# PEER picks split between VectorE and ScalarE, a shorter top-16 and an earlier first list of ids

## The reference, cut to what matters

```python
def peer(h, w_query, keys1, keys2, exp_u, exp_v):
    q = (h @ w_query).reshape(T, PEER_HEADS, 2, D_PHALF)
    s1 = jnp.einsum('thd,nd->thn', q[:, :, 0], keys1)
    s2 = jnp.einsum('thd,nd->thn', q[:, :, 1], keys2)
    v1, i1 = lax.top_k(s1, 16)
    v2, i2 = lax.top_k(s2, 16)
    cand_s = v1[..., :, None] + v2[..., None, :]          # 16 x 16 sums
    cand_i = i1[..., :, None] * 128 + i2[..., None, :]
    top_s, sel = lax.top_k(cand_s, 16)
    e_idx = jnp.take_along_axis(cand_i, sel, axis=-1)
    gate = jax.nn.softmax(top_s, axis=-1)
    u = exp_u[e_idx]
    act = jax.nn.gelu(jnp.einsum('thkd,td->thk', u, h))
    return jnp.einsum('thk,thkd->td', gate * act, exp_v[e_idx])
```

## Time and profile before

| | |
|---|---|
| median of three runs | 1144.43 us |
| profiled execution, its own time | 1144.88 us |
| its span, from the first to the last instruction | 1143.1 us |
| TensorE busy | 856.5 us (75%) |
| VectorE busy | 784.8 us (69%) |
| ScalarE busy | 454.8 us (40%) |
| GpSimd busy | 536.3 us (47%) |
| mean granted clock of TensorE | 0.902 |
| moved by the DMA engines | 456.60 MB, 402.68 MB of it by the gathers |

### The profile page before, as it was taken

How to read it: one execution, slowest core, us unless ns; L and a number is a source line. 1 busy time by engine, 2 the same in 40 slices (tenths; PEclk the granted TensorE clock), 3 DMA queues, 4 the chain that set the end, 5 groups by cost and what they waited for, 6 DMA issues and landing times.

```text
span 1143.1 us, 12068 instructions
## 1 busy us (share of the span) xinstructions
PE 856.5 (75%) x3879; PEld 396.3 (35%) x3884; DVE 784.8 (69%) x2005; ACT 454.8 (40%) x1423; POOL 536.3 (47%) x437
## 2 busy tenths in 40 slices
PE   8999988997896858685686777587666756655555
PEld 6748743443232424241243442143223222211111
DVE  2325877876677888796666786757877777667554
ACT  2121454333444334552564663343343333333334
POOL 0002445553555554553553553556564654455442
PEclk9999999999999888897889898889898788887879
DMA  9902999999999999999999999999999999999996
GB/s 375 411 2 70 421 425 425 427 424 430 425 427 425 426 428 426 361 430 422 425 427 425 425 427 427 425 426 427 426 427 426 427 427 428 427 425 427 427 428 269
DMA packets 66791, 456.60 MB, mean 399 GB/s; under 512 B 8227, under 2 KB 10019, under 8 KB 15526
## 3 DMA queue, kind: packets, MB, share of 16 engines
q0 software_dynamic: 55888, 402.68, 83.8%
q1 hardware_dynamic: 10694, 52.87, 11.4%
q10 hardware_dynamic: 144, 0.26, 0.1%
HBM read 451.49 MB, written 3.24 MB: 398 GB/s over the span
## 4 chain that ended last, share of the span: by engine, by line
DMA 48%; PE 26%; DVE 11%; POOL 7%; ACT 4%; issue 3%; SPq 0%; POOLq 0%; DVEq 0%
DMA rows<-in_uv,ids 37%; PE ps L598 25%; DMA wt<-in_uv,ids 8%; DVE rows L2043 6%; POOL rows L537 4%; POOL work L520 2%; DMA wt<-in_uv,last_ids 1%; DMA rows<-in_w_qi 1%; ACT work L1249 1%; ACT wt L1249 1%; DMA wt<-in_w_q 1%; ACT wgt L1249 1%; DVE wt L2043 1%; PE ps L601 1%; ACT zact L1249 1%
## 5 line engine op out<-in xcount | busy, mean ns | idle before, releaser
L537 POOL DMA_INDIRECT rows<-in_uv,ids x352 | 400.3, 1137 | 444.9 <-PE ps L598 360.7
L598 PE MATMUL ps<-rows,work 128*64 128x512 f32 x1416 | 409.4, 707 | 245.2 <-ACT work L1249 239.7
L2043 DVE CUSTOM_DVE_ANT_0 rows<-rows,wt 128x1024 f32<-128x1024 f32 x226 | 276.9, 1225 | 160.9 <-DMA rows<-in_uv,ids 155.7
L1249 ACT ACTIVATE zact<-zdot 128x1 f32<-128x1 f32 x354 | 71.6, 202 | 488.2 <-DVE zdot L2043 480.5
L598 PEld LDWEIGHTS ps<-rows,work 128*64 128x64 f32 x1416 | 96.2, 151 | 479.3 <-ACT work L1249 327.3
L598 PE MATMUL ps<-wt 128*128 128x128 f32 (+6 forms) x719 | 195.9, 476 | 30.4 <-ACT wt L1249 28.1
L2043 DVE CUSTOM_DVE_ANT_0 rows<-rows,masks 128x1024 f32<-128x1024 f32 x128 | 156.3, 1224 | 67.3 <-DMA rows<-in_uv,ids 64.5
L598 PEld LDWEIGHTS ps<-wt 128*128 128x128 f32 (+2 forms) x724 | 97.8, 185 | 106.6 <-issue 58.8
L1249 ACT ACTIVATE work<-pair,wgt 128x64 f32<-128x64 f32 x354 | 123.4, 349 | 11.5
L1249 ACT ACTIVATE wgt<-zact,gates 128x1 f32<-128x1 f32 x354 | 104.5, 295 | 11.6
L598 PEld LDWEIGHTS ps<-work,wt 128*128 128x128 f32 (+1 forms) x664 | 84.2, 202 | 48.6 <-issue 48.2
(11 more groups left out here) (178 smaller groups left out, 722.9 us busy)
## 6 DMA issues: line engine op xcount, KB each, us to landing
wt<-in_w_q SPq DMA_DIRECT2D x7, 2048.0 KB, 15.9
rows<-in_uv,ids POOLq DMA_INDIRECT x352
rows<-in_w_out SPq DMA_DIRECT2D x2, 2048.0 KB, 32.5
wt<-in_w_out SPq DMA_DIRECT2D x2, 2048.0 KB, 12.0
wt<-in_ckv SPq DMA_DIRECT2D x16, 256.0 KB
x<-in_x SPq DMA_DIRECT2D x5, 512.0 KB, 8.9
rows<-in_w_qi SPq DMA_DIRECT2D x1, 2048.0 KB, 13.3
wt<-in_w_qa SPq DMA_DIRECT2D x1, 2048.0 KB, 12.5
```

The costliest lines, as they stand in the source:

```text
L537: pool.indirect_dma_start(row[s], None, a["uv"], bass.IndirectOffsetOnAxis(ap=ids[:, own(n // KP).start + n % KP:own(n // KP).start + n % ...
L598: return nc.tensor.matmul(out, lhsT, rhs, start=start, stop=stop)
L1249: return nc.scalar.activation(*args, **kw)
L2043: V.tensor_tensor_reduce(row[s][:, 0:D], row[s][:, 0:D], h2r[t][:, n % 2, :], 1.0, 0.0, ALU.mult, ALU.add, zdots[s]).then_inc(dotted, 1)
```

## The change

There are three parts.

1. *Picks 250 to 378, the even ones (65 of them).* VectorE runs a plain multiply of two 128x1024 tensors and no accumulator read. ScalarE, at the head of `weigh`, runs a Copy over the 1024 products with an accumulator, waits for it, and goes on with the gelu. `gelus(n)` counts the semaphore for it.
2. *Top-16 of every unit.* The two casts to fp32 go. The index of the first half is shifted left by 7 bits while it is an integer; the place among the 256 candidates is split into its two nibbles by one AND with the constants 240 and 15 (set once at the start) in place of a shift, an AND and a cast; the comparison constants are 0, 16, 32 ... for the first half and 0, 1, 2 ... for the second; and one reduction over both halves gives the id, where a reduction to two half ids and a multiply-add gave it. `post` signals a semaphore and yields, with no wait after.
3. *Unit 0.* Its ids signal `chosen` on their own, ahead of the softmax. `spread_first` spreads the ids with 4 matmuls and then the gates with 4, each of 8 columns; `spread_take(0)` signals `picked` after the ids, and takes the gates when they are there. All later counts of `chosen`, `spread_ps` and `picked` are one higher.

```diff
-    c["iota"] = np.broadcast_to(np.arange(KP), (P, KP))
+    c["iota"] = np.broadcast_to(np.concatenate([np.arange(KP) * KP, np.arange(KP)]), (P, 2 * KP))
...
+        def summed_by_act(n):
+            return 250 <= n < 380 and n % 2 == 0
+
+        def gelus(n):
+            return n + 1 + sum(summed_by_act(k) for k in range(n + 1))
...
-                    pool.wait_ge(picked, n // KP + 1)
+                    pool.wait_ge(picked, n // KP + 2 if n else 1)
...
+            def spread_first():
+                pe.wait_ge(q_sb, 1)
+                for k in range(2):
+                    pe.wait_ge(chosen, k + 1)
+                    for j in range(2):
+                        for q in range(2):
+                            last = mm(spread_psum(k)[64 * q:64 * q + 64, j * KP + k * 8:j * KP + k * 8 + 8], ident[:, 64 * j:64 * j + 64],
+                                      flat[0].rearrange("p e (c q) -> p e q c", q=2)[:, k, q, :])
+                    last.then_inc(spread_ps, 1)
...
-            spread_out(0)
+            spread_first()
...
+                if summed_by_act(n):
+                    A(row[s][:, 0:D], row[s][:, 0:D], ACT.Copy, accum_out=zdots[s]).then_inc(gelued, 1)
+                    act.wait_ge(gelued, gelus(n) - 1)
                 A(zacts[s], zdots[s], ACT.Gelu).then_inc(gelued, 1)
-                act.wait_ge(gelued, n + 1)
+                act.wait_ge(gelued, gelus(n))
...
+            def post(ins, s):
+
+                key = s.name
+                count[key] = count.get(key, 0) + 1
+                ins.then_inc(s, 1)
+                yield
...
-                then(V.tensor_copy(topf, topi))
                 c4 = cand.rearrange("p (i j) -> p i j", i=KP)
                 yield from across(V.tensor_tensor(c4, top[:, 0, :].rearrange("p (i a) -> p i a", a=1).broadcast_to([P, KP, KP]),
                                                   top[:, 1:2, :].broadcast_to([P, KP, KP]), ALU.add))
-                then(V.max(out=best[:, 0:8], in_=cand))
+                V.max(out=best[:, 0:8], in_=cand).then_inc(chain, 1)
+                V.tensor_scalar(topi[:, 0, :], topi[:, 0, :], 7, None, ALU.logical_shift_left).then_inc(chain, 1)
+                count[chain.name] += 2
+                dve.wait_ge(chain, count[chain.name])
...
-                V.tensor_scalar(rank[:, 0, :], besti, 4, None, ALU.logical_shift_right)
-                then(V.tensor_scalar(rank[:, 1, :], besti, 15, None, ALU.bitwise_and))
-                yield from across(V.tensor_copy(rankf, rank))
-                yield from across(V.tensor_tensor(hot, rankf.rearrange("p e (k a) -> p e k a", a=1).broadcast_to([P, 2, KP, KP]),
-                                                  iota[:].rearrange("p (e a r) -> p e a r", e=1, a=1).broadcast_to([P, 2, KP, KP]),
+                yield from across(V.tensor_tensor(rank, besti.rearrange("p (e k) -> p e k", e=1).broadcast_to([P, 2, KP]),
+                                                  nibble.rearrange("p (e k) -> p e k", k=1).broadcast_to([P, 2, KP]), ALU.bitwise_and))
+                yield from across(V.tensor_tensor(hot, rank.rearrange("p e (k a) -> p e k a", a=1).broadcast_to([P, 2, KP, KP]),
+                                                  iota.rearrange("p e (a r) -> p e a r", a=1).broadcast_to([P, 2, KP, KP]),
                                                   ALU.is_equal))
-                yield from across(V.tensor_tensor(hot, hot, topf.rearrange("p e (a r) -> p e a r", a=1).broadcast_to([P, 2, KP, KP]),
+                yield from across(V.tensor_tensor(hot, hot, topi.rearrange("p e (a r) -> p e a r", a=1).broadcast_to([P, 2, KP, KP]),
                                                   ALU.mult))
-                yield from across(V.tensor_reduce(half_id, hot, AX.X, ALU.add))
-                V.scalar_tensor_tensor(flat[u % 2][:, 0, :], half_id[:, 0, :], float(NK), half_id[:, 1, :], ALU.mult, ALU.add).then_inc(chain, 1)
-                count[chain.name] += 1
+                ids_of = V.tensor_reduce(flat[u % 2][:, 0, :], hot.rearrange("p e k r -> p k e r"), AX.XY, ALU.add)
+                if u == 0:
+                    ids_of.then_inc(chosen, 1)
+                else:
+                    yield from post(ids_of, chain)
                 dve.wait_ge(gexp, u + 1)
...
-                dve.wait_ge(spread_ps, u + 1)
+                dve.wait_ge(spread_ps, u + 2 if u else 1)
                 src = spread_psum(u).rearrange("p (j e c) -> p e c j", j=2, e=2)
-                V.tensor_copy(ids[:, own(u)].rearrange("p (c j) -> p c j", j=2), src[:, 0, :, :])
-                if u >= 1:
-                    dve.wait_ge(picked, u)
+                ins = V.tensor_copy(ids[:, own(u)].rearrange("p (c j) -> p c j", j=2), src[:, 0, :, :])
+                if u == 0:
+                    ins.then_inc(picked, 1)
+                    dve.wait_ge(spread_ps, 2)
+                    src = spread_psum(1).rearrange("p (j e c) -> p e c j", j=2, e=2)
+                dve.wait_ge(picked, u + 1)
                 V.tensor_copy(gates[:, own(u)].rearrange("p (c j) -> p c j", j=2), src[:, 1, :, :]).then_inc(picked, 1)
...
-                V.tensor_tensor_reduce(row[s][:, 0:D], row[s][:, 0:D], h2r[t][:, n % 2, :], 1.0, 0.0, ALU.mult, ALU.add,
-                                       zdots[s]).then_inc(dotted, 1)
+                if summed_by_act(n):
+                    V.tensor_tensor(row[s][:, 0:D], row[s][:, 0:D], h2r[t][:, n % 2, :], ALU.mult).then_inc(dotted, 1)
+                else:
+                    V.tensor_tensor_reduce(row[s][:, 0:D], row[s][:, 0:D], h2r[t][:, n % 2, :], 1.0, 0.0, ALU.mult, ALU.add,
+                                           zdots[s]).then_inc(dotted, 1)
```

More of the change, by code:

```diff
@@ L101, in build @@
         m16 = sb("m16", [P, STEPS])
-        iota = sb("iota", [P, KP])
         half4 = sb("half4", [P, HB])
@@ L253, in build @@
         topi = at(work, 3968, 32).bitcast(U32).rearrange("p (e k) -> p e k", e=2)
-        topf = at(work, 4000, 32).rearrange("p (e k) -> p e k", e=2)
+        nibble = at(work, 4000, 2).bitcast(U32)
         best = at(work, 4032, KP)
@@ L257, in build @@
         rank = at(work, 4064, 32).bitcast(U32).rearrange("p (e k) -> p e k", e=2)
-        rankf = at(work, 4096, 32).rearrange("p (e k) -> p e k", e=2)
-        half_id = at(work, 3840, 32).rearrange("p (e k) -> p e k", e=2)
+        iota = at(work, 4096, 32).rearrange("p (e k) -> p e k", e=2)
         ebest = at(work, 3808, 2 * KP).rearrange("p (b k) -> p b k", b=2)
@@ L406, in _ @@
             for name, dst in (("e8", e8), ("bar", bar), ("pair", pair[:]), ("m16", m16[:]),
-                              ("iota", iota[:]), ("kd", kd[:]), ("cs", at(masks, 1536, 384)), ("dmask", at(masks, 0, 1024))):
+                              ("iota", at(work, 4096, 32)), ("kd", kd[:]), ("cs", at(masks, 1536, 384)), ("dmask", at(masks, 0, 1024))):
                 sp.dma_start(dst, a[name]).then_inc(small_in, 16)
@@ L814, in query_part @@
                     if u == 1:
-                        pe.wait_ge(picked, 1)
+                        pe.wait_ge(picked, 2)
                     k = q_load(u)
@@ L840, in query_scores @@
                 if u >= 2:
-                    pe.wait_ge(picked, u if u - 1 in AHEAD else u - 1)
+                    pe.wait_ge(picked, u + 1 if u - 1 in AHEAD else u)
                 pe.wait_ge(q_sb, u + 1)
@@ L845, in query_scores @@
                 last.then_inc(sc2_ps, 1)
+            def spread_first():
[7 more added lines that the diff above has]
+                    last.then_inc(spread_ps, 1)
             def spread_out(u):
[L848 to L851, removed]
+                pe.wait_ge(chosen, u + 2)
+                if u not in AHEAD:
                     pe.wait_ge(topped, min(u + 2, UNITS))
@@ L1657, in row_max @@
                     dve.wait_ge(expd, step)
-                yield from across(V.tensor_scalar(negmax[:, c:c + w], rowmax[:, c:c + w], -(DH ** -0.5), None, ALU.mult), smax)
+                yield from post(V.tensor_scalar(negmax[:, c:c + w], rowmax[:, c:c + w], -(DH ** -0.5), None, ALU.mult), smax)
             def scale_probs(step, prob, c, w):
@@ L1663, in scale_probs @@
                 shape = [P, w, prob.shape[2]]
-                yield from across(V.tensor_tensor(prob, prob, resum[:, c:c + w].rearrange("p (j a) -> p j a", a=1).broadcast_to(shape),
-                                                  ALU.mult), pscaled)
+                yield from post(V.tensor_tensor(prob, prob, resum[:, c:c + w].rearrange("p (j a) -> p j a", a=1).broadcast_to(shape),
+                                                ALU.mult), pscaled)
             def rotate(t, bank, cs, scratch):
@@ L1728, in top16_halves @@
                     if u >= 1 and e == 1:
-                        dve.wait_ge(chosen, u)
+                        dve.wait_ge(chosen, u + 1)
                     ins = V.max(out=top[:, e, 0:8], in_=s[e])
@@ L1818, in _ @@
             then(V.memset(ident_bf[:], 0.0), blank)
```

(3 more changed lines are left out.)

2 lines of the change are left out of this document (1 added, 1 removed).

## The result

The changed kernel takes 1157.14 us (median of 4 runs, 1156.7 to 1158.15) against 1144.98 us before (4 runs, 1144.29 to 1145.9): a ratio of 1.0107, with an interval of 1.0089 to 1.0124. It is 12 us slower, where 1143.7 us and a range up to 1145.9 were forecast. The profiled execution took 1156.7 us, its span 1154.8 us.

A forecast was written before the change was run, and what follows sets the result against it. The prediction took the picks to be bound by row transfers at 427 GB/s; 0 + 0 + 0.3 (middle pause) + 0.4 (start) = 0.7 us off 1144.88 gave 1144.2, or 1143.7 us as median, range 1141.8 to 1145.9.

The forecast's parts named there:

- The step that failed: Whole kernel: with picks bound by transfers, only an earlier stream start or shorter pauses were priced; all else 0.
- the whole sum: All edits: 0 for sums, 0 for later top-16s, 0.3 us middle pause, 0.4 us start; 0.7 us gained.
- What bounds the kernel: Picks: bound by transfer of their rows, 1.05 MB at 427 GB/s, 2.46 us each; DMA share 1.01 in the last third.
- The rival of a slower DMA rate: 806 to 1125 us: ScalarE's sums slow gathers from 427 to 423 GB/s, costing 3.0 us, 1146.7 us; 7%.
- The sums and the later top-16s at 0: 65 picks and 23 units: VectorE saves 5.4 us by sums, about 0.5 us a unit, all hidden beside transfers: 0.
- The plain product: VectorE, 65 even picks: a multiply without accumulator read takes 1.225 us, like the fused one, saving about 0.083 us a pick.
- the bound of twice the speed: Upper bound for the product on VectorE: 44 us saved over 65 picks, still worth 0 in time.
- The middle pause: 461 to 478 us: 1.7 us without a transfer, expected to shrink by 0.3 us (bounds 0 and 1.7).
- The second pause that the prediction had as a lower bound: Middle of the kernel: one more such pause could appear as the waiting pick shifts, -1.7 us.
- The start: Unit 0: first gather at 109.2 instead of 109.65, 0.45 us earlier, pick 4 unmoved; 0.4 us taken (bounds 0 and 0.6).
- VectorE done long before: Expected sign in unit 0: the ids' spread starts when TensorE's sums end, at 108.2, with VectorE finished well ahead.
- The second four matmuls then fill the idle time that is gone: TensorE, unit 0: gates' matmuls use the former idle time, so its next sums still start at 108.98 to 109.0.

The follow-up runs named there:

- the padded kernel: The changed kernel plus an unused tensor of 64 bytes per partition where `iota` stood, so `rows` and all behind it lie as before: 1141.85 us.
- the three kernels with the old order at 427 GB/s: Old top-16: the kernel before; it with `wt` 64 bytes off and `rows` aligned (1144.97 us); it with ScalarE's sums alone (1143.55 us).
- the four with the new one: New top-16: the padded kernel; it with slots at multiples of 512 (1142.02 us); without sums (1143.07); without sums and ids not ahead (1142.94).

## Why the prediction was wrong

*The step that failed* is the one behind the whole sum: "All else in the sum is how much earlier the stream starts or how much less it pauses." It took the rate, 427 GB/s, for a property of the machine that only other traffic could disturb, and so priced instructions and waits alone. The rate also depends on where the tensors lie in a partition: 427 GB/s with `rows` at a multiple of 256 bytes, 420 or 421 with it off. The diff changed that in a line that the prediction gave no term at all, the allocation of `iota`. The missing term was +14.9 to 15.3 us, against 0.7 us for the whole sum. Because the gathers bound the kernel, as the prediction said, a loss of 1.4% in the rate went into the time undiminished.

*What bounds the kernel*: right. The DMA share is 1.01 after as before, and the pairs wait for landings.

*The rival of a slower DMA rate* had the right sign and symptom, "a DMA rate below 425 behind 806 us", and the wrong cause: at 427 GB/s in the padded kernel with all sums in it, ScalarE's 0.5 MB read and written per sum cost the transfers nothing. Its price was made for 423 GB/s over 320 us; it was 421 over the whole stream, from 141 us on. The window 141:200 (419 against 426 GB/s) rules the sums out with no experiment, since none runs there. The Trainium skill, SBUF — State Buffer, "SBUF: two separate sides", holds here with a number: 427 GB/s at 188 us of ScalarE's work and at 116.

*The sums and the later top-16s at 0*: no cost, as forecast, but not 0 either. "All of it is work in front of a wait for a landing [...], so it is worth 0 at either bound" is off by 0.84 us for the sums, and the same reasoning by 0.85 us for the top-16s behind pick 250. *The plain product* at 1.23 us: right; the bound of twice the speed was not needed.

*The middle pause*: 0.3 us was taken from 1.7. The 1.7 was read from the DMA share, and it was too small: the bytes of the same window, 327 of 427 GB/s, make it 17 x (1 - 327/427) = 4.0 us, so near a pause the share hides more than half of it. How much shorter the pause became can't be read from one window, as it moves: the kernels with the old order and the slots off, whose instructions are those of the kernel before, show shares from 0.93 to 0.97 in 461:478. From VectorE's start on pick 0 to its start on pick 250 it is 685.2, 685.4 and 685.9 us in the three kernels with the old order at 427 GB/s, and 684.0, 684.0, 684.4 and 685.0 in the four with the new one. The means differ by 1.2 us, single executions by 0.2 to 2.0. The second pause that the prediction had as a lower bound did come, in some: the 29 us around 390 us fall to 408 GB/s in the padded kernel, 398 without its sums, and 386 in the changed one, but also to 400 and 385 in two kernels with the old order (`iota` behind `wt`, and 128 above).

*The start*: 0.45 us for the first gather and none for pick 4 were worked out. Counted from the first instruction of unit 0's choice, 0.59 and 0.27 us came. "VectorE done long before" was right for the ids, which end at 106.25 + 0.69 = 106.94 us, 0.7 before the spread starts at 107.65; for the gates, whose product ends at 107.24 + 0.23 = 107.47, it is 0.2. "The second four matmuls then fill the idle time that is gone, so TensorE starts its next sums where it did" was wrong by 0.27: from the start of the sums ahead (107.07) to the sums behind the spread (108.98) it was 1.91 us, and 108.22 - 106.59 = 1.63 after.

*The edits together* bring 2.7 us (by the interval of the ratio 1.4 to 3.4 us) where 0.7 was forecast. Between the profiled executions of the kernel before and the padded one, 2.5 us of span apart, 0.6 lie ahead of pick 0 (0.3 of them because unit 0's choice starts earlier in that execution), 0.2 between pick 0 and pick 250, and 1.7 between pick 250 and pick 383; behind it nothing changes. So most of the gain lies where the prediction had 0. That the padded kernel's 1141.85 us falls into the forecast's range (from 1141.8) is luck: it is at its edge, by gains that the sum did not have.

## What to carry to other kernels

Where a kernel is bound by transfers, write down the start of every buffer that they land in before and after a change, modulo 256 bytes; a small tensor added or removed ahead of it is then a part of the change. A pad of 64 bytes was enough here. In a profile compare GB/s, not only the DMA share: a lower rate at an equal full share, in a stretch that the edits do not touch, points at the transfers, and in a pause the share hides a part of what the bytes show. Before a loss is put down to an edit, run the kernel before with the new addresses. Where a start drifts by half a microsecond between executions, measure from a point ahead of the edit; where pauses elsewhere scatter, measure between two numbered steps of the loop.

## What the runs showed of the hardware

Gathers with 8192 bytes to each partition move 427 GB/s when all slots start at a multiple of 256 bytes in a partition of SBUF and 420 or 421 when all start 64, 128 or 192 bytes above one, at a DMA share of 1.01 in both. On a time of 1144.5 us that is 15.3 to 15.9 us. A multiple of 512 gives no more. The starts are the allocator's; in distances, the slots moved down by 0 or 256 bytes are fast, and by 64, 128 or 192 slow. With two of the ten slots 64 above and the other eight aligned it stays at 427, and those two slots' gathers cost next to nothing (0.13 us for 27 of them, where 1.0 would be their share). So the loss is not a price of each transfer by its own destination.

The grain of 256 bytes is also that of the Trainium skill, DMA: Bandwidth & Descriptors, "How a descriptor splits into AXI transactions": a transaction starts at a multiple of 256 bytes, and a transfer that doesn't start there costs extra beats. The page says this of the reads, with one beat for 32 bytes fetched in vain. An estimate by its count for 8192 bytes is 2, 4 or 6 beats more than 256 at offsets of 64, 128 and 192, so 0.8, 1.6 and 2.3%. The runs, which moved the destinations alone, show 1.4% at each and nearly nothing for the two slots off by themselves, so they don't bear out that count for the destination's side. What the loss comes from stays open. Whether an unaligned source row costs anything, what an offset of 32 bytes does, and what `rows` and the small tensors ahead of it do each by itself, wasn't tried.
